# Expert pairs in one loop from the second batch on, and residual rows added inside the first batch

## The reference

```python
def one_block(args):
    toks, e = args
    xb = x_pad[toks]
    hb = jax.nn.silu(xb @ w1[e]) * (xb @ w3[e])     # w1, w3: 1024 x 256
    return hb @ w2[e]                               # w2: 256 x 1024

y_rows = lax.map(one_block, (row_tok.reshape(n_blk, MOE_BLOCK), blk_exp)).reshape(n_rows, D)
y = jax.ops.segment_sum(y_rows * row_gate[:, None], row_tok, num_segments=T + 1)[:T]
```

## Time and profile before

| | us |
|---|---|
| median of 3 runs | 1147.37 |
| lowest, highest | 1146.15, 1149.80 |
| profiled execution, time | 1149.87 |
| profiled execution, span | 1148.10 |
| PE busy in the span | 1042.9 (91%) |
| DVE busy | 403.4 (35%) |
| ACT busy | 262.5 (23%) |
| DMA moved | 441.03 MB, mean 384 GB/s |

### The profile page before, as it was taken

The page is one execution under the profiler, slowest core; times in us unless marked ns, Lnnn a source line. Parts: engine busy times, 40 slices in busy tenths (PEclk is TensorE's granted clock), DMA queues, the critical chain, the costliest instruction groups (busy, mean ns, idle before and its releaser), DMA issues.

```text
span 1148.1 us, 26594 instructions
## 1 busy us (share of the span) xinstructions
PE 1042.9 (91%) x11334; PEld 532.8 (46%) x11334; DVE 403.4 (35%) x1189; ACT 262.5 (23%) x682; POOL 18.7 (2%) x36
## 2 busy tenths in 40 slices
PE   9999999888989988888999999898999899888888
PEld 5665744443444434333466657354444444333333
DVE  4865432222232222121268656232222222222213
ACT  1245312211122111111132543122111111111111
POOL 0010000000000000000000100000000000000000
PEclk9999999999999999999999999999999999999999
DMA  9967699999999999999996677999999999999996
GB/s 307 334 245 293 255 403 427 426 426 428 426 428 429 429 428 429 429 429 421 388 310 212 264 297 286 416 427 427 426 427 427 429 428 426 428 429 428 429 421 250
DMA packets 72860, 441.03 MB, mean 384 GB/s; under 512 B 16480, under 2 KB 36064, under 8 KB 43616
## 3 DMA queue, kind: packets, MB, share of 16 engines
q1 hardware_dynamic: 72512, 439.52, 93.4%
q0 software_dynamic: 144, 0.58, 0.1%
q10 hardware_dynamic: 144, 0.07, 0.0%
HBM read 439.10 MB, written 1.05 MB: 383 GB/s over the span
## 4 chain that ended last, share of the span: by engine, by line
PE 84%; DVE 6%; DMA 5%; issue 3%; SPq 1%; ACT 1%; another core or an unknown queue 0%; POOL 0%; DVEq 0%
PE bank L1171 15%; PE bank L1086 15%; PE bank L1183 10%; PE bank L693 8%; PE bank L1068 8%; PE bank L1101 4%; DMA w_odd<-in_moe_w 4%; PE bank L819 4%; PE bank L1136 3%; PE bank L1055 2%; PE bank L1177 2%; DVE moe L1742 2%; DVE moe L1713 1%; PE bank L963 1%; DMA w_even<-in_w_in 1%
## 5 line engine op out<-in xcount | busy, mean ns | idle before, releaser
L1809 ACT ACTIVATE moe<-bank 128x512 f32<-128x512 f32 (+2 forms) x164 | 84.1, 523 | 551.0 <-PE bank L1086 276.1
L1713 DVE COPY moe<-bank 128x512 f32<-128x512 f32 x64 | 44.3, 692 | 311.0 <-PE bank L1086 258.0
L1183 PE MATMUL bank<-moe 128*128 128x512 f32 (+1 forms) x264 | 119.3, 593 | 22.8 <-DVE moe L1742 21.7
L1171 PE MATMUL bank<-w_even,moe 64*32 64x512 f32 x896 | 100.7, 599 | 10.0 <-DVE moe L1734 10.0
L1068 PE MATMUL bank<-moe,x 128*64 128x64 f32 x3072 | 98.2, 224 | 4.8 <-issue 4.8
L1086 PE MATMUL bank<-w_even,moe 64*32 64x512 f32 x1536 | 91.3, 620 | 11.5 <-issue 11.5
L1068 PEld LDWEIGHTS bank<-moe,x 128*64 128x64 f32 x3072 | 94.6, 138 | 9.1 <-issue 9.1
L1086 PE MATMUL bank<-w_odd,moe 64*32 64x512 f32 x1536 | 87.7, 598 | 8.6 <-DMA w_odd<-in_moe_w 6.2
L1171 PE MATMUL bank<-w_odd,moe 64*32 64x512 f32 x768 | 86.9, 600 | 7.4 <-DVE moe L1734 7.4
L1742 DVE COPY moe<-bank 128x512 f32<-128x512 f32 x32 | 22.1, 691 | 199.3 <-PE bank L1171 181.5
L1183 PEld LDWEIGHTS bank<-moe 128*128 128x128 f32 x264 | 47.2, 189 | 93.6 <-DVE moe L1742 46.2
(11 more groups left out here) (205 smaller groups left out, 1006.2 us busy)
## 6 DMA issues: line engine op xcount, KB each, us to landing
w_even<-in_moe_w SPq DMA_DIRECT2D x76, 2048.0 KB, 36.6
w_odd<-in_moe_w SPq DMA_DIRECT2D x72, 2048.0 KB, 33.8
w_odd<-in_moe_w SPq DMA_DIRECT2D x44, 1024.0 KB, 10.1
w_even<-in_moe_w SPq DMA_DIRECT2D x40, 1024.0 KB, 9.8
w_even<-in_w_in SPq DMA_DIRECT2D x24, 768.0 KB, 10.9
w_odd<-in_w_out SPq DMA_DIRECT2D x4, 2048.0 KB, 13.6
w_odd<-in_moe_w SPq DMA_DIRECT2D x8, 512.0 KB, 11.7
w_even<-in_w_in SPq DMA_DIRECT2D x4, 416.0 KB, 6.9
```

Source lines behind the costliest of these rows:

```text
L1171: last = mm(bank[h][BLK * k:BLK * (k + 1), :], hT_pair[rows, c, BLK * q:BLK * (q + 1)], w2_pairs[parity][q][rows, c, 512 * h:512 * h + 512 ...
L1183: return mm(Y[t][h][:, lo - 512 * h:hi - 512 * h], scatter[:, t * P:(t + 1) * P], y_rows[:, lo:hi], start=start, stop=True, skip_group_che ...
L1713: nc.vector.tensor_copy(partial[:, k, :], source[:, :]).then_inc(part_dve.sem, 1)
L1809: return fn(dst, src, ACT.Copy)
```

## The change

From batch 1 to batch 14 every batch is paired and runs in one loop of two (odd, then even). Batch 15 has its w1 and w3 in pairs too, with the gate half of its second pair multiplied ahead of the up half; its w2 stays as it was. Batch 0 stays plain. SP's list changes with it: what was loaded for batch 1 as eight DMAs of 1 MB for w1 and w3 and four of 1 MB for w2 becomes four and two of 2 MB, and the first w2 load of batch 1, which stood behind `upT_psum`, goes with the second behind `ropT_psum`. Batch 2's w1 and w3 come in pairs, the first of them in two halves.

The seeds move into batch 0 and ahead of it: tile 0 is turned (`turn_rows(0)`) right after the first half of the first gather, into its own `Y` banks, and scaled by ACT alone (8 activations), and added between experts 1 and 2 of batch 0. Tile 1 is turned after expert 3, scaled by ACT and DVE (4 each), and added while the hidden rows are copied. `keep_warm` there goes from 11 to 7. `seed_rows` now starts the sums in `Y`, and `add_rows` never does.

```diff
         zb = moe_mem[:, 2 * DM:3 * DM], moe_mem[:, DM:2 * DM]
-        seed_mem = moe_mem[:, 0:DM].rearrange("p (c t) -> p c t", c=DC)
+        seed_mem = moe_mem[:, DM:2 * DM].rearrange("p (c t) -> p c t", c=DC)
         c0 = part(NT * C0).rearrange("p (t n) -> p t n", t=NT)
...
                 after(sp, l, comb, 4)
-                load_w13(0, 0, 0)
-                load_w13(0, 1, 0)
-                after(sp, l, upT_psum, 2)
-                load_w2(1, 3, 1)
+                load_w13(0)
+                load_w13(1)
                 after(sp, l, comb, 8)
-                load_w13(0, 2, 0)
-                load_w13(0, 3, 0)
+                load_w13(2)
+                load_w13(3)
                 load_w_out(0)
 
                 after(sp, l, s_psum, 10)
-                load_w13(1, 3, 1)
+                load_w13_pair(1, 1, 1, 1)
                 after(sp, l, ropT_psum, 8)
-                load_w2(1, 2, 1)
+                load_w2_pair(1, 1, 1)
 
                 after(sp, l, prod, 20)
                 load_w_out(1)
                 after(sp, l, comb, 11)
                 for k in range(3):
-                    load_w2(0, k, 0)
+                    load_w2(k)
 
 
                 after(sp, l, o_psum, PAIRS)
-                load_w13(1, 2, 1)
+                load_w13_pair(1, 1, 0, 1)
 
                 after(sp, l, x_ready, 4)
-                load_w2(0, 3, 0)
+                load_w2(3)
 
                 after(sp, l, mix_psum, 3)
-                load_w13(1, 1, 1)
+                load_w13_pair(1, 0, 1, 1)
                 after(sp, l, mix_psum, 5)
...
-                        if by_matrix and k == 0:
-                            after(sp, l, gate_first, 1)
-                            load_w13(e, k, parity, matrices=(0,))
-                        done = 2 * (k // 2) + 2 if last else k + 1
-                        sp.wait_ge(part_psum.sem, (b0 + j) * NB + (part_psum.start + done - back))
-                        plain(sp)
...
-                    else:
-                        load_pairs(j, back, e, parity)
+                            load_w13_pair(e, q, m_, parity)
                     sp.wait_ge(y2_psum.sem, (b0 + j) + (y2_psum.start + 1 - back // NB))
                     plain(sp)
 
 
-                load_first(2, 2 * NB, 2, 0, by_matrix=True)
+                after(sp, l, gate_first, 1)
+                load_w13_pair(2, 0, 0, 0, slice(0, DC))
+                first_batch_used(1)
+                load_w13_pair(2, 0, 0, 0, slice(DC, 2 * DC))
+                first_batch_used(2)
+                load_w13_pair(2, 0, 1, 0)
+                first_batch_used(3)
...
@@ -532,7 +530,7 @@
                         load_w2_pairs(j & (BATCHES - 1), parity)
                 load_batch(m, 2 * NB, BATCHES - 2, 0)
                 load_w2_pairs(BATCHES - 2, 0)
-                load_batch(m, NB, BATCHES - 1, 1, True)
...
                             rows = slice(64 * h, 64 * h + 64)
                             last = mm(Y[t][h].rearrange("p (d c) -> p c d", c=DC)[:, c, :], seed_mem[rows, c, :],
-                                      ident[rows, rows], start=False, stop=True, is_transpose=True,
...
                 after(pe, l, n_ready, 1)
                 after(pe, l, chosen_first, 1)
                 gather_first(0)
-                keep_warm(11, bank[7])
+                turn_rows(0)
+                keep_warm(7, bank[7])
                 after(pe, l, picked, 2)
...
+                                      skip_group_check=True)
+                            if m_ and c == 2 * DC - 1:
+                                last.then_inc(part_psum.sem, 1)
+                    return last
+
+                def up_gate(k):
+                    pe.wait_ge(w13_in[0][k].sem, b0 * 8 + (32 + 16 * l))
+                    w = w13_slots[0][k]
                     if k >= 2:
-                        pe.wait_ge((part_dve if k % 2 == 0 else part_act).sem, b * 2 + 1)
+                        pe.wait_ge((part_dve if k % 2 == 0 else part_act).sem, b0 * 2 + 1)
                     for c in range(DC):
-                        if k == 0 and c == 4:
-                            pe.wait_ge(xg_act.sem, b + 1)
...
-                def turn_hidden(b):
+                def turn_hidden(b, meanwhile=None):
                     hc = hn.rearrange("p (f c) -> p c f", c=2)
                     pe.wait_ge(hn_ok.sem, b + 1)
                     for c in range(2):
                         last = nc.tensor.transpose(bank[1][:, SEQ + c * P:SEQ + (c + 1) * P], hc[:, c, :], ident)
                     last.then_inc(hT_psum.sem, 1)
+                    if meanwhile:
+                        meanwhile()
                     pe.wait_ge(hT_sb.sem, b + 1)
 
...
                 def first_batch():
                     first_up_gate()
-                    up_gate(0, 0, 1, 32 + 32 * l)
...
+                    seed_rows(0)
+                    up_gate(2)
+                    up_gate(3)
+                    turn_rows(1)
                     pe.wait_ge(part_dve.sem, b0 * 2 + 2)
                     pe.wait_ge(part_act.sem, b0 * 2 + 2)
                     fold(bank[0], slice(0, 2 * FE)).then_inc(gu_psum.sem, 1)
                     pe.wait_ge(gated_ok.sem, b0 + 1)
                     turn_gated(bank[1])
...
                     pe.wait_ge(scT_sb.sem, b0 + 1)
-                    turn_hidden(b0)
-                    all_down(0, 0)
...
+                    turn_hidden(b0, lambda: seed_rows(1))
+                    first_down()
                     pe.wait_ge(y2_dve.sem, b0 + 1)
                     pe.wait_ge(y2_act.sem, b0 + 1)
-                    add_all(True)
-
-                def batch(j, parity, seen=None, pairs=True, next_pairs=True, seeds=None):
-                    b = b0 + (j + parity)
+                    add_all()
+
+                def batch(j, parity):
+                    b = b0 + j
                     pe.wait_ge(xg_dve.sem, b + 1)
-                    if seen is None:
...
                 def last_batch(j):
-                    b = b0 + (j + 1)
+                    b = b0 + j
                     pe.wait_ge(xg_dve.sem, b + 1)
-                    for k in range(NB - 1):
-                        up_gate(j, 1, k, 48 + 32 * l)
+                    up_gate_pair(j, 1, 0)
+                    pair_in(j, 1, 2)
+                    plain(pe)
+                    up_or_gate_pair(0).then_inc(gate_part_psum.sem, 1)
                     pe.wait_ge(gated_ok.sem, b + 1)
-                    turn_gated(bank[3])
...
-                    after(pe, l, w1_last_in, 16)
                     pe.wait_ge(part_act.sem, b * 2 + 1)
-                    up_or_gate(0, bank[1]).then_inc(gate_part_psum.sem, 1)
-                    keep_warm(2, bank[2])
+                    turn_gated(bank[1])
+                    pe.wait_ge(part_dve.sem, b * 2 + 1)
+                    after(pe, l, gate_part_dve, 1)
+                    after(pe, l, gate_part_act, 1)
+                    fold(bank[0], slice(0, FE)).then_inc(gate_psum.sem, 1)
+                    pair_in(j, 1, 3)
+                    plain(pe)
+                    up_or_gate_pair(1)
+                    pe.wait_ge(scT_sb.sem, b + 1)
                     pe.wait_ge(part_dve.sem, b * 2 + 2)
-                    after(pe, l, gate_part_sb, 1)
-                    fold(bank[0], slice(0, FE)).then_inc(gate_psum.sem, 1)
-                    pe.wait_ge(w13_in[1][NB - 1].sem, (b0 + j) * 8 + (32 + 16 * l))
-                    up_or_gate(1, bank[2]).then_inc(part_psum.sem, 1)
-                    pe.wait_ge(scT_sb.sem, b + 1)
                     pe.wait_ge(part_act.sem, b * 2 + 2)
...
                 first_batch()
-                batch(0, 1, 32 + 32 * l, pairs=False, next_pairs=False, seeds=0)
-                batch(2, 0, 48 + 32 * l, seeds=1)
-                batch(2, 1)
-                with pe.Fori(4, m, 2) as j:
-                    batch(j, 0)
+                with pe.Fori(1, m, 2) as j:
                     batch(j, 1)
-                batch(m, 0, next_pairs=False)
-                last_batch(m)
+                    batch(j + 1, 0)
...
 
-                def scale_seeds(t):
+                def seeds(t, chunks):
+                    after(act, l, n_ready, 2)
                     after(act, l, seed_psum, t + 1)
-                    for c in range(4, DC):
-                        last = fn(seed_mem[:, c, :], bank[3][:, c % 4 * P:(c % 4 + 1) * P], ACT.Identity,
+                    for c in chunks:
+                        last = fn(seed_mem[:, c, :], Y[t][c // 4][:, c % 4 * P:(c % 4 + 1) * P], ACT.Identity,
                                   scale=g_cols[:, 0, c:c + 1], bias=g_cols[:, 1, c:c + 1])
...
+                def copy_gathered(g):
```

More of the change, by code:

```diff
@@ L1698, in _, with take @@
                 m, b0 = start_batches(v, base, l)
-                def batch(j, last_of_all, e_next, first=False, pairs=False, w13_pairs=False, next_pairs=False,
-                          seeds=None):
-                    b = b0 + j
-                    def choose_next():
```

(23 more changed lines are left out.)

303 lines of the change are left out of this document (148 added, 155 removed).

## The result

The changed kernel takes 1151.77 us (median of 6 runs, 1150.62 to 1153.33); its ratio to the kernel before is 1.0035, 95% interval [1.0024, 1.0046], so 4 us (0.35%) slower. Timed again on another occasion it gave 1.0021 [1.0009, 1.0032], 2.4 us. The forecast was +2.2 us on the profiled execution and 1149.2 us in all: the sign and the range held, the middle was 2.6 us low. That the total came near is luck in part. The loss is small because one cost, larger than forecast, met a gain of 4 us that the forecast didn't have.

A forecast was written before the change was run, and what follows sets the result against it. Each layer's expert weight stream bounds, PE outside it. Terms +3.5 + 0.3 + 0 + 0 - 1.6 = +2.2 us on the median 1147.37 give 1149.6, with the clock 1149.2 us; range 1144.8 to 1153.2.

The forecast's parts named there:

- `w_out` half 1 behind 1 MB more: Attention's output projection: half 1 lands 2.45 us later, PE waits 2.3 us in layer 0, 1.2 in layer 1: +3.5 us.
- the rule that the forecast went by: Loads ahead of `w_out` half 1: each DMA engine consumes one issuer's descriptors in ring order, so 2.45 us count in full.
- ACT's eight scalings and PE's turns ahead of batch 0: Ahead of batch 0: scalings covered by ACT's gather wait, cost nothing; PE's turns less four `keep_warm` +0.13 us a layer, +0.3 in all.
- PE in batches 0 to 14: Expert stages: PE reaches batch 4 some 3.7 us later against the stream; waits of 7.66 us absorb it, cost 0.
- The waits for weights: PE's waits in batches 11 to 14 become shorter by as much as batch 1 becomes longer, about 5 us.
- SP's refill, cover 1.8 us: SP's batch 3 issue, after batch 2's loads: some 3 us later relative to the stream, 1.8 us of cover left, holds narrowly.
- The stream: Each layer's expert weights at 428 GB/s: ends a fixed time after it starts, so its length does not change.
- The last batch: Batch 15: up fold starts 1.0 us earlier; about 0.6 us remain in layer 1, 1.0 in layer 0: -1.6 us.
- The third down product's weights: Last batch, layer 1: weights land at 1131.8, PE is there at 1130.9 and waits 0.9 us.
- The clock: Products behind batch 14's wait: half clock costs 1.7 us a layer; -3.4 us if both drops go, 0 if both stay.
- Rival 2: Attention: PE waits for `w_out`, then runs at half clock, 1.7 us more in each layer: 1153.0 us; chance 0.15.
- The sum: Whole kernel: +3.5 + 0.3 + 0 + 0 - 1.6 = +2.2 us, 1152.1 on the profiled execution, 1149.6 on the median.

The follow-up runs named there:

- the second profile: Profile of the changed kernel run again without an edit; that run measured 1150.03 us, ratio 1.0021 to the kernel before.
- the move alone: Kernel before, with only batch 1's early 1 MB w2 load (expert 3) moved to just ahead of `w_out` half 1's load: 1153.30 us, ratio 1.0043.
- The swap: Changed kernel with `w_out` half 1's load issued ahead of batch 1's 2 MB w2 load instead of behind it: 1145.61 us, ratio 0.9976.
- The runs with batches written out: PE's batches ahead of its loop: 1 to 4 in changed kernel, 1.0074; with `w_out` half 1 issued first, 1 to 4 1.0011, 1 and 2 1.0008.
- the filler: Changed kernel with `w_out` half 1 issued first, plus 2 `keep_warm` matmuls ahead of the second pair in batches 1 to 14: 1144.82 us, ratio 0.9971.
- the wait filled 12, 5: Changed kernel with 12 `keep_warm` matmuls in layer 0 and 5 in layer 1 ahead of `w_out` half 1's first product: 1151.16 us, ratio 1.0023.
- the kernel before with the same swap: Kernel before, with `w_out` half 1's load issued ahead of the 1 MB w2 load that stood before it: 1148.37 us, ratio 1.0006.

## Why the prediction was right or wrong

*`w_out` half 1 behind 1 MB more, +3.5 us (2.3 and 1.2).* Right in mechanism and place, too small. The waits were 2.84 and 1.43 us, in the second profile 2.85 and 1.24, and the move alone cost 4.9 us (+-1.6). The step that failed in size is the landing: 2.45 us were added to the earlier trace rows, and 2.9 and 2.7 came. That the two transfers queue, the rule that the forecast went by, is borne out by these landings: 1 MB more in front, at the same place in SP's list, made half 1 land later by a little more than that megabyte's own time. The swap shows that the place costs the time, but not by the queue alone: half 1 was also issued 4.3 us earlier there, free of the wait for `ropT_psum`.

*ACT's eight scalings and PE's turns ahead of batch 0, +0.3.* Right that nothing of weight is there: ACT has 0.49 us of cover left. From the last run of output products, which half 1's are part of (it starts at 105.22 in the profile of before, 105.12 in that of the kernel with `w_out` first), to the first refill it is 42.73 us before and 42.56 there: -0.2, not +0.3. The two profiles of the changed kernel add to it what the waits explain, +4.6 us (2.84 of wait, 1.70 of half clock) and +2.9 (2.85).

*PE in batches 0 to 14, nothing.* The 0 is right, the way to it is not. PE's down product of batch 2 comes 63.73 us after the first refill, against 59.66 before: 4.1 us later, as forecast (3.7). But by batch 4 it is 0.5 us earlier (115.81 against 116.29) and by batch 6 2.5 us earlier (167.88 against 170.39). The waits for weights were to be 5 us shorter; they are 8.7 us in layer 0 before and after. What the forecast missed is time that PE lost before, in batches run from code that was new to it. Three waits inside the gather (total, times, longest) are gone in the changed kernel. Each ended 2.4 to 2.5 us after the start of a code fetch:

```profile
PE bank L1068 <- issue: 4.8, 3, 1.7
```

The down product of batch 4 took 8.77 us besides, where 7.07 is usual. That the stream's waits take up PE work is shown by the filler: 6.8 us more a layer vanished in them.

*SP's refill, cover 1.8 us.* Right as far as it goes: no gap in DMA from 156 us on. Between 152 and 156 the rate is 246 to 324 GB/s, at the stream's start; before it was 201 at 148 to 150 and 315 at 152 to 154.

*The stream, no change.* The forecast let it end "a fixed time after it starts". Wrong, and the largest miss: -2.5 and -1.5 us, -4.0 in all (-3.9 in the second profile). It had counted fresh code as PE time only, though the page of before has a queue line of 45 instruction packets. The runs with batches written out show the price by themselves.

*The last batch, -1.6.* The mechanism held, the size did not: 0.64 us shorter in layer 1 from start to down product, where 1.0 had been worked out, because the up fold started 9.14 us after the batch did and not 8.8 (the gate fold and the up half took 0.64 and 2.00 us, where 0.5 and 1.8 had been reckoned); and the gather for it, now in pairs, costs 0.42 us more (3.99 against 3.57), less 0.15 of the turn behind it, a term I left out. Net -0.3 to -0.4 a layer, -0.7 in all, read from the traces and not isolated by a run. The third down product's weights, which were to bind in layer 1, didn't in either profile of the changed kernel. They do where the tail runs at full clock behind a wait of 1.6 us: by 0.53 us with `w_out` first and by 0.45 with the wait filled 12, 5.

*The clock.* Rival 2 came true in one of two profiles, for layer 0 only: +1.7 us. The drops in the tails stayed in both, as in the earlier trace rows.

*The sum.* By the profiles, without what comes and goes: the waits +4.1 to +4.3, ahead of batch 0 -0.2, the stream -4.0, the last batch -0.7 make -0.7. The measured +2.4 to +4.0 us is higher. The stream of before is overstated in this: its 378.71 us in layer 0 is the longest of the three profiles with its code, the shortest being 377.86. Against that one the stream gave only 1.7 + 1.4 us, and the sum is +0.2. The half clock and the late fetch at the end (1.7 and 1.6 us, each in one of two profiles) make up part of the rest. One or two us are not resolved, as large as the intervals; the run with the small load late, too, cost 1.1 us more than its waits. So the prediction's total was right with two misses of opposite sign in it, the stream by 3 to 4 us one way and the waits, the last batch, the clock and the unresolved rest the other. The kernel with `w_out` first fits better: -0.2 - 2.9 - 0.7 = -3.8, measured -2.8 (+-1) to the kernel before and -3.4 to the kernel before with the same swap.

## What to carry to other kernels

Where a stream of loads sets the time, look at what else uses the DMA engines, code above all. Loads land with the slowest of 16 engines, so a batch written out ahead of a loop can cost more than its instructions save; the spread of a load's 16 completions shows what it cost so far. When a load is made larger or moved, look first at which load is queued behind it and when that one is needed; here swapping two issues turned a loss of 0.2 to 0.35% into a gain of 0.24%. And where PE waits for the stream, it has room: work put in front of such a wait was free, until the next load bound.

## What the runs showed of the hardware

- A code fetch (16 KB, 0.9 to 1.1 us long) in a full stream costs the loads some 0.2 to 0.4 us on average, five to ten times the 0.04 us of its bytes over 16 engines (16 KB at 428 GB/s). In 24 stretches from 376.1 to 380.3 us the stream's length follows the spread of its last load, 2.0 to 6.1 us, to within 0.8 us; a lag is kept to the end of the stream.
- Code that runs for the first time can also stop PE: in the kernel before, three waits of 1.4 to 1.7 us in layer 0, each with a code fetch started 2.4 to 2.5 us before PE went on.
- One fetch stood among the last writes of the output where the program's end came 1.6 us later. It came in one of two profiles of the same kernel, at 1148.1; in the other the last fetch stood at 1137.5.
- The clock's drop is not set by the length of PE's wait alone. Ahead of half 1 it fell to 0.50 behind 2.84 us, and behind 2.85 us at the same place it did not fall. Ahead of batch 14's second pair the twelve profiles have 16 waits of 3.06 to 3.19 us; behind ten of them the 64 records took 5.2 to 5.5 us, behind six 3.7. Behind the five waits of 1.46 to 1.65 us they took 3.7 each time.
